# Streaming the columns of every three-product matmul from last to first in a two-block transformer kernel

## The reference, cut to what matters

```
for l in range(2):
    proj = rmsnorm(x) @ w_in[l]            # q, k, v, conv inputs, two gates
    merged = sigmoid(ga) * attention(q, k, v) + sigmoid(gb) * conformer_conv(u, ug)
    x = x + merged @ w_out[l]
    g, up = split(rmsnorm(x) @ w_gate_up[l])
    x = x + (silu(g) * up) @ w_down[l]
# second block, once: retention and a spatial gating unit in place of attention
# and convolution, then out projection, a gated MLP with a width-3 convolution,
# and a down projection, each followed by an rmsnorm of its output
```

## Time and profile before

| | |
|---|---|
| median of the runs | 2197.57 us |
| span of the profiled execution | 2195.6 us |
| TensorE matmuls, busy | 2182.7 us (99%) |
| TensorE weight loads, busy | 1813.8 us (83%) |
| VectorE busy | 1378.5 us (63%) |
| ScalarE busy | 965.5 us (44%) |
| mean granted TensorE clock | 0.999 |

### The profile page before, as it was taken

How to read it: one execution, slowest core, us unless ns; L and a number is a source line. 1 busy time by engine, 2 the same in 40 slices (tenths; PEclk the granted TensorE clock), 3 DMA queues, 4 the chain that set the end, 5 groups by cost and what they waited for, 6 DMA issues and landing times.

```text
span 2195.6 us, 28930 instructions
## 1 busy us (share of the span) xinstructions
PE 2182.7 (99%) x10528; PEld 1813.8 (83%) x10528; DVE 1378.5 (63%) x1978; ACT 965.5 (44%) x1392; POOL 74.7 (3%) x103
## 2 busy tenths in 40 slices
PE   9999999999999999999999999999999999999998
PEld 6878888888888878888888888888888899888887
DVE  7999954444345999954444334654776568888723
ACT  5678544443223588544443223331554344333412
POOL 0000020000010000020000010000000000000000
PEclk9999999999999999999999999999999999999999
DMA  5221222222223211222222224223222231222222
GB/s 182 75 78 65 96 96 96 96 96 84 93 93 123 90 62 64 94 96 100 99 99 92 80 92 156 97 77 131 84 91 87 96 135 39 100 101 97 94 96 77
DMA packets 35397, 208.39 MB, mean 95 GB/s; under 512 B 4512, under 2 KB 5024, under 8 KB 14816
## 3 DMA queue, kind: packets, MB, share of 16 engines
q1 hardware_dynamic: 35296, 207.07, 27.0%
HBM read 201.15 MB, written 2.10 MB: 93 GB/s over the span
## 4 chain that ended last, share of the span: by engine, by line
PE 94%; ACT 3%; DVE 2%; issue 1%; DMA 0%; SPq 0%; DVEq 0%
PE mm L1794 25%; PE mm L1796 25%; PE mm L1795 25%; PE sp L1794 4%; PE sp L1795 4%; PE sp L1796 4%; PE sp L1896 1%; PE ob L1924 1%; DVE conv_y L1171 1%; ACT probs L584 1%; DVE probs L1201 1%; ACT probs L592 1%; PE sp L1911 0%; DMA x<-in_x_dram 0%; PE ob L1796 0%
## 5 line engine op out<-in xcount | busy, mean ns | idle before, releaser
L1794 PE MATMUL mm<-in_hi,w_hi 128*128 128x512 f32 (+1 forms) x1696 | 663.8, 391 | 3.8 <-DVE in_lo L1104 2.1
L1796 PE MATMUL mm<-in_hi,w_lo 128*128 128x512 f32 (+1 forms) x1696 | 657.0, 387 | 0.0
L1795 PE MATMUL mm<-in_lo,w_hi 128*128 128x512 f32 (+1 forms) x1696 | 657.0, 387 | 0.0
L525 ACT ACTIVATE w_hi<-w_raw 128x2048 fp32r<-128x2048 f32 (+3 forms) x193 | 346.2, 1794 | 674.8 <-PE mm L1796 557.9
L1070 DVE TENSOR_TENSOR w_lo<-w_raw,w_hi 128x2048 fp32r<-128x2048 f32 (+3 forms) x193 | 422.3, 2189 | 239.5 <-ACT w_hi L525 239.0
L1794 PEld LDWEIGHTS mm<-in_hi,w_hi 128*128 128x128 f32 x1696 | 318.5, 188 | 75.1 <-DVE in_lo L1104 6.0
L1796 PEld LDWEIGHTS mm<-in_hi,w_lo 128*128 128x128 f32 x1696 | 318.4, 188 | 65.8
L1795 PEld LDWEIGHTS mm<-in_lo,w_hi 128*128 128x128 f32 x1696 | 318.6, 188 | 64.1 <-issue 1.0
L1171 DVE SCALAR_TENSOR_TENSOR conv_y<-conv_in,parl,conv_y 128x512 f32<-128x512 f32 x240 | 170.0, 747 | 1.7
L1081 DVE TENSOR_TENSOR tB<-mm,rstd 128x512 f32<-128x512 f32 x54 | 37.3, 691 | 172.8 <-PE mm L1796 172.8
L1794 PE MATMUL mm<-act_hi,w_hi 128*128 128x512 f32 x352 | 136.9, 389 | 0.0
(11 more groups left out here) (429 smaller groups left out, 3257.0 us busy)
## 6 DMA issues: line engine op xcount, KB each, us to landing
w_raw<-in_w_dram SPq DMA_DIRECT2D x160, 1024.0 KB, 4.8
w_raw<-in_w_dram SPq DMA_DIRECT2D x32, 704.0 KB, 3.9
w_raw<-in_w_dram SPq DMA_DIRECT2D x5, 512.0 KB, 4.7
out_dram<-z_rows SPq DMA_DIRECT2D x8, 256.0 KB, 2.1
rope<-in_rope_dram SPq DMA_DIRECT2D x3, 512.0 KB, 3.6
x<-in_x_dram SPq DMA_DIRECT2D x4, 256.0 KB, 4.9
x<-in_x_dram SPq DMA_DIRECT2D x2, 512.0 KB, 7.9
sq<-ssum SPq DMA_DIRECT2D x32, 32.0 KB, 1.8
```

Of the source, the lines that this page charges most:

```text
L525: e.activation(whi[:, slot, 0:cols], raw[:, slot, 0:cols], ACT.Copy).then_inc(s_whi, whi_out.up())
L1794: MM(out, ah, bh, start=first, stop=False, **kw)
L1795: MM(out, ah, bl, start=False, stop=False, **kw)
L1796: return MM(out, al, bh, start=False, stop=last, **kw)
```

## The change

Ahead of the three matmuls, `mm3` turns `out`, `bh` and `bl` round: an operand with two dimensions gets its columns in reverse order, one with three gets both free dimensions reversed. So the first column streamed is the last of the moving operand, and its result goes to the last column of the output. Each address step along the columns becomes minus one element. The pairing of columns, the products, the sums and the memory that is read and written stay the same, and so do the number of matmuls, the stationary operand, the semaphores and everything outside `mm3`.

```diff
@@ -1791,9 +1791,10 @@
 
             def mm3(out, ah, al, bh, bl, first, last, **kw):
 
-                MM(out, ah, bh, start=first, stop=False, **kw)
-                MM(out, ah, bl, start=False, stop=False, **kw)
-                return MM(out, al, bh, start=False, stop=last, **kw)
+                back, bh, bl = (t[:, ::-1] if len(t.shape) == 2 else t[:, ::-1, ::-1] for t in (out, bh, bl))
+                MM(back, ah, bh, start=first, stop=False, **kw)
+                MM(back, ah, bl, start=False, stop=False, **kw)
+                return MM(back, al, bh, start=False, stop=last, **kw)
```

## The result

The changed kernel takes 2247.39 us (median of 2247.32 and 2247.47), against 2197.57 us before: 49.8 us more, a ratio of 1.0227 with a 95% interval from 1.0197 to 1.0257. The profiled execution has a span of 2245.7 us, 50.1 us longer than before.

A forecast was written before the change was run, and what follows sets the result against it. TensorE was taken to bound the kernel. The edit's terms summed to 0 us, so 2195.6 us of span plus 2.0 us around it gave 2197.6 us; the stated range was 2190 to 4150 us.

The forecast's parts named there:

- half rate: Rival in the memory path of each mm3 matmul: reversed steps handle one column in two cycles; 1925 us more, 4123 us; chance 0.27.
- What bounds the kernel: Step on the whole span: TensorE alone sets the time, busy 2182.7 of 2195.6 us; additions to matmuls lengthen it almost one for one.
- The output written down, and the last column first: Steps on mm3's output: writing with step minus one, and column 511's result coming before column 0's, were both taken to cost nothing.
- The moving operand read down: Step on mm3's moving operand: reading it with a step of minus one, 9504 times, was taken to cost nothing.
- the argument on neighbours: Reason for zero cost in mm3: successive columns are memory neighbours either way, so aligned units get the same runs of accesses.
- The bound below: Lower limit on the cost in mm3's matmuls: nothing gained, since 512 columns already take 512 cycles at full clock.
- The fixed price: Rival at each mm3 matmul's start: rate kept, one more 13.3 ns gap; 126 us more, 2324 us; chance 0.06.
- The bound by plain float32: Upper limit on the cost in mm3: matmuls at the pace of L1817's plain float32 product, 0.86 us each, 5739 us more.
- The chances: Odds for the whole kernel's time: within 2% 0.61, slower by over 2% 0.37, faster 0.02.

## Why the prediction was right or wrong

The time lies in the stated range, but near its lower end and not where I had put it: the forecast of 2197.6 us missed by 49.8 us, and its own range of 2190 to 2208 did not hold. That the wide range holds the time is luck: it reached up to 4150 us for the half rate, which isn't what happened. By its own steps:

**What bounds the kernel** held. Of the 54.8 us that the paces add, 50.1 us came out in the span; VectorE and ScalarE didn't matter. The counts, 8544 and 960, and their paces were right. That the 13.3 ns beyond 0.417 ns for each column are a fixed part of every matmul was not: 480 columns upwards took 216.7 ns and not 213.3.

**The output written down, and the last column first**: priced at nothing, measured at nothing (2197.47 us for the write alone).

**The moving operand read down**: priced at nothing, and this is the step that failed. It measured 6.6 ns for each of the 8544 long matmuls and -1.7 ns for each of the 960 short ones. The reason I gave, that reversal changes the order and not the set of what is touched and that a memory would have to look at the sign of the step, looked at one stream by itself. For small units that is even true: swapped pairs and groups of 4 cost nothing, and two halves in the wrong order neither. But the order of the 16-byte groups mattered, and the argument on neighbours had ruled that out. What it also left out stood in the paragraph ahead of it: the weight load as "the second read stream" that "isn't touched". The trace had the row, two reads of the same memory in the same interval, and I took their overlap for independence; the upward runs show that the two operands' places relative to each other set the pace.

**The bound below**, nothing gained, was wrong for the 256-column matmuls, which became 1.7 ns faster.

**The rivals.** Half rate was given 0.27 and is far off: no run showed anything like 440 ns, the worst was 266.7. Its argument, that a step other than plus one halves the rate on the way to a memory, is answered by the write, which ran down for nothing, and by the read, which paid 6.6 ns of 226.7. The fixed price was given 0.06 and came nearest in form, an addition of some ns to each matmul, at 13.3 ns where 6.6 was right. But its mechanism, a setup that each reversed stream pays, is refuted by the pairs and the halves, and by the short matmuls. The term is mis-sized by a factor of two, and its cause was another. I sized it by a gap in the trace that no run ties to it. The bound by plain float32 has a slip that nothing hangs on: 0.86 - 0.227 is 0.633 us and not 0.636, so about 5717 us and not 5739.

**The chances.** 0.61 lay on within 2% and 0.37 on more; the ratio of 1.0227 has an interval that reaches down to 1.0197, so the case is at the border.

What is shown: the price of the full reversal is on the read side; a price sets in when neighbouring 16-byte groups follow each other downwards; and with all reading upwards the place of moving and stationary operand relative to each other can bring one of the same size. What is only argued: that the two prices are one and the same thing, that the partner is the weight load of the next matmul, and that the two meet in some division of the memory by address. Against the first speaks that the shift by 64 bytes left the downward 233.3 ns as they were. For the weight load speaks that moving the stationary tensor changes the pace, and that the price falls in the interval in which that load starts. Open are why the price of full reversal is 6.6 ns at two different relative places and 40 ns for blocks of 16, whether those 40 ns belong to the reading, why the short matmuls gain, and whether some place makes the downward read free. Reversing the stationary operand as well, which might let both run the same way, wasn't tried.

## What to carry to other kernels

Ask of a change of order or place not only what its own stream does, but which other stream reads the same memory in the same interval; a matmul's moving operand and the next weight load may be such a pair. Where TensorE is the bound and reads upwards, look at the byte place of moving and stationary tensors relative to each other. Multiples of 512 bytes are what the kernel before has; 256 bytes were as good on the one tensor tried; 64 bytes off cost this kernel 46.3 us, 2.1%, in a version that looks the same in every other respect. Writing to PSUM from last to first, and the order within 16 bytes, cost nothing here.

## What the runs showed of the hardware that was not expected

- A 512-column float32r matmul of the kernel before takes 226.7 ns from start to start only because its operands lie well: 231.7 to 236.5 ns when the moving one is 16 to 128 bytes lower, 226.7 again at 256 bytes.
- Walking 16 columns down, then the next 16, in moving operand and output costs 266.7 ns, more than any other order tried, full reversal (233.3) included.
- Fewer columns don't save in proportion: 480 columns took 216.7 ns and 512 took 226.7, where 32 columns at 0.417 ns are 13.3.
- Reversed reading makes 256-column matmuls faster, 118.3 against 120.0 ns, and so does a moving operand 64 bytes lower with all reading upwards, 115.4 ns.
- The pace of a group can depend on the group ahead of it: in two places the first six long matmuls took up to 236 ns before they settled at 226.7.
